# Twelve conditioning chunks split seven and five, and the last recurrent head's tail rearranged, in a one-layer diffusion backbone

## The chip, the cores and the metric

The kernel runs on one core of a Trainium2 chip. The metric is the device time of one execution in microseconds (us); the median of several executions counts.

## The reference, cut to what matters

One trunk layer is computed for 128 context tokens and 1024 latent tokens (1152 columns in all, in nine tiles of 128). The part around the change is this:

```python
mod = (silu(cond) @ ada_w + ada_b).reshape(2, 6, 1024)      # cond: c_ctx and c; ada_w is 1024 x 6144, 24 MB
sh1, sc1, g1, sh2, sc2, g2 = mod[:, 0..5]
h = rmsnorm(x, norm1) * (1 + sc1) + sh1                      # needs sh1 and sc1 only
aq, ak, av, rq, rf_f, rf_b, ri, rg, za, zr = split(h @ w_in)
# eight recurrent heads (HGRN2, both directions), key and value size 128
o_rec = rmsnorm(o_f + o_b, r_gain) * silu(rg)
merged = sigmoid(za) * attention + sigmoid(zr) * o_rec
x = x + g1 * (merged @ w_o)
h = rmsnorm(x, norm2) * (1 + sc2) + sh2                      # sh2, sc2, g2: used much later
x = x + g2 * conv_ffn(h)
```

## The kernel before, in words

Four phases follow one another, each in a block of its own with a barrier at its end: `phase0` (conditioning and the normalised, modulated, transposed input), `phase1` (eight recurrent heads), `phase2` (attention and output projection), `phase3` (the convolutional feed-forward part). Activations and weights are kept as a high part and a low part, and each projection is three matmul passes (lines 336 to 338) of 384 columns.

**Phase 0.** `ada_w` arrives in twelve chunks of 512 columns, 2 MB each, in three buffers (`AW`, line 177). A chunk's buffer is filled again when TensorE has read it. `columns(c)` (line 235) multiplies the two silu'd conditioning vectors, padded with zeros to 32 columns, by the chunk, 8 row blocks into four groups of 32 PSUM partitions. ScalarE copies the result to `mod_rows` (`MR`, line 215), and `rows(c)` (line 245) turns it by four tiny matmuls against `row_select` into columns of the modulation, which VectorE adds to the bias (line 300). Chunks 0 to 3 hold shift and scale of the first norm, chunks 4 to 11 the rest. From chunk 4 on, each chunk comes with one of the eight 128-row blocks of x (a "column" of x here), in three parts of 1, 4 and 4 token tiles: TensorE transposes the part (`x_part`, line 253), VectorE scales and shifts it into `h_f32` (`HF`, line 320), ScalarE rounds it to `act_hi` (`HH`, line 219), and VectorE subtracts to make `act_lo` (`HL`, line 312). ScalarE does the copy of chunk c (line 215) before the three parts that go with it. GpSimd splits the first three weight blocks (lines 188 and 190), which SP loads behind chunk 9 and at the end (lines 180 and 182). All of this is in written order on each engine, held together by semaphores.

**Phase 1.** The first head's six projection units (`unit(0, u)`, 18 groups of 24 matmuls) run on TensorE with nothing between them. GpSimd first clears the semaphores of phase 0 (`spent`, line 478 on) and then releases TensorE by adding to `w_split`. `gates(0)` on VectorE (lines 746 to 760) turns the forget gates into decays and writes `q_dec` and `k_dec`. Then a loop does the recurrence of head r between the projections of head r + 1. The last head has no projections beside it. Its tail: nine tiles of scores, masks (lines 795 to 801) and outputs; ScalarE copies each output tile to `rec_out` and its square to `SQ` (lines 647 and 648); three groups of 384 tokens are summed over the partitions by a matmul with ones (line 580), rooted on ScalarE (line 652), inverted on VectorE (line 812), multiplied into `rec_out` with the gain (line 814) and then with the gate (line 816). The gate is silu(rg) times sigmoid(zr), a product of 1152 columns on VectorE (line 805). One DMA stores all of `rec_out` (line 444), and the phase ends when it has landed.

Of the kernel before, what the change touches and what calls it, by code (L numbers as in the profile page):

```python
# [14 lines left out]
P = 128  # L15
D = 1024
KC = D // P
# [47 lines left out]
def build(nc, a, outs):  # L65
# [9 lines left out]
    with ExitStack() as ctx:  # L75
# [25 lines left out]

        W = (sb("w_raw", [P, 2, KC, P]), sb("w_hi", [P, 3, KC, P], F32R), sb("w_lo", [P, 3, KC, P], F32R))
        phase0(nc, a, sb, pb, sem, W, w_in, (B_RQ, B_RFF, B_RFB), HH, HL, ident, ones, CW, MOD, A1, A2, lb, lb1, lb1n, rgain)

        spent = sems[:]
        phase1(nc, a, sem, W, w_in64, HH, HL, ident, ones, lb, lb1, lb1n, rgain, w_in, rec_dram, out_state, spent)
# [7 lines left out]
def phase0(nc, a, sb_, pb_, sem, W, w_in, first_units, HH, HL, ident, ones, CW, MOD, A1, A2, lb, lb1, lb1n, rgain):  # L114

    with ExitStack() as ctx:
# [4 lines left out]
        NCOL = 12  # L121
# [8 lines left out]
        HF = sb("h_f32", [P, 2, 512])  # L130
# [3 lines left out]
        SEL = sb("row_select", [P, 2])  # L134
# [17 lines left out]
        xt_done, hf_done, hi_done, lo_done = sem("xt_done"), sem("hf_done"), sem("hi_done"), sem("lo_done")  # L152
# [3 lines left out]
        EARLY = 4  # L156
        X_FOR = {c: range(3 * (c - EARLY), 3 * (c - EARLY) + 3) for c in range(EARLY, NCOL)}
        ada = a["ada_w"][0].rearrange("(k p) (b c) -> b p k c", p=P, c=512)

        with nc.Block() as block:  # L160
            @block.sync
            def _(sp):
# [11 lines left out]
                for c in range(NCOL):  # L174
                    if c >= AHEAD:
                        sp.wait_ge(ada_done, c - AHEAD + 1)
                    sp.dma_start(AW[:, c % AHEAD], ada[c]).then_inc(ada_in[c % AHEAD], 16)
# [15 lines left out]
            def _(act):  # L193
# [5 lines left out]
                act.wait_ge(vec_ok, 1)  # L199
                nc.scalar.activation(SG[:, :], VT[:, 64:80], ACT.Sigmoid).then_inc(cond_sig, 1)  # L200
                act.wait_ge(vec_ok, 2)
                nc.scalar.activation(lb[:, :], LD[:, :], ACT.Sigmoid).then_inc(cond_sig, 1)
                for t in range(NT):
                    if t % 3 == 0:
# [5 lines left out]
                nc.scalar.activation(RS[:, :], SS[:, :], ACT.Sqrt).then_inc(sqrt_done, 1)  # L210
                for c in range(NCOL):
                    act.wait_ge(ada_done, c + 1)
# [3 lines left out]
                    for n in X_FOR.get(c, ()):  # L216
                        j, (t0, t1, _) = n // 3, GR[n % 3]
                        act.wait_ge(hf_done, n + 1)
                        nc.scalar.activation(HH[:, j, t0 * P:t1 * P], HF[:, n % 2, 0:(t1 - t0) * P], ACT.Copy).then_inc(hi_done, 1)

            @block.tensor
            def _(pe):
# [15 lines left out]
                def rows(c):  # L238
                    pe.wait_ge(ada_out, c + 1)
                    if c >= EARLY:  # L240
                        pe.wait_ge(vec_ok, 2)
                        pe.wait_ge(lo_done, 1)
                    out = mps if c < EARLY else vps
                    for b in range(4 * c, 4 * c + 4):
                        m = nc.tensor.matmul(out[:, 2 * b:2 * b + 2], MR[:, c % 2, (b - 4 * c) * P:(b - 4 * c + 1) * P], SEL[:, :], start=True, stop=True)
                    m.then_inc(mod_t, 1)

                def x_part(n):
                    j, (t0, t1, _) = n // 3, GR[n % 3]
                    if n >= 4:  # L250
                        pe.wait_ge(hf_done, n - 3)
# [6 lines left out]
                for c in range(1, EARLY):  # L258
                    columns(c)
                    rows(c - 1)  # L260
                rows(EARLY - 1)
                pe.wait_ge(xn_done, NT)
                for c in range(EARLY, NCOL):
                    for n in X_FOR[c]:
                        x_part(n)
                    columns(c)
# [2285 lines left out]
```

## Time and profile before

| | us |
|---|---|
| median of three runs | 2728.85 |
| lowest and highest | 2724.72, 2728.87 |
| the profiled execution, its own time | 2727.76 |
| its span in the profile | 2725.7 |
| TensorE busy (matmul) | 2586.0 (95%) |
| VectorE busy | 1705.9 (63%) |
| ScalarE busy | 1027.3 (38%) |
| GpSimd busy | 826.3 (30%) |

The profile is of one execution. Times in it are us from the start of the span, "busy" leaves out waiting, and a bracket at the end of a row of the timeline tells how long the engine had been idle and what released it. The matmuls are pipelined, so that the next one starts before the last one's end: the distance from start to start is what a matmul costs in a stream.

### The profile page before, as it was taken

How to read it: one execution, taken by the hardware profiler on the slowest of the kernel's cores; microseconds unless marked ns; L12 is line 12 of the kernel's file. 1: busy time of each engine (PE TensorE's matmuls, PEld its weight loads, DVE VectorE, ACT ScalarE, POOL GpSimd, SP SyncE). 2: the span in 40 equal slices, each digit the busy share in tenths (PEclk: the TensorE clock that was granted, in tenths of full speed). 3: DMA queues.
4: the chain of work that ended last, by engine and by line, in shares of the span. 5: the costliest groups of instructions: out<-in, count | busy, mean ns of one | idle time of the engine just before them, and what ended most of it. 6: DMA issues, size and time to landing. Idle time of an engine off the chain costs nothing. (4 is left out here: it accounts for less than half of the span.)

```text
span 2725.7 us, 40115 instructions
## 1 busy us (share of the span) xinstructions
PE 2586.0 (95%) x14417; PEld 2386.3 (88%) x14417; DVE 1705.9 (63%) x2809; ACT 1027.3 (38%) x1915; POOL 826.3 (30%) x775
## 2 busy tenths in 40 slices
PE   6899999999997999999999999799999999999997
PEld 2799999999997977778778676699999999999997
DVE  3247456546748367777677666437766777667675
ACT  3233323323323256666666657433122211222214
POOL 0222132223222433433433323624223222232222
PEclk8899999999999999999999999899999999999999
DMA  9411111111110200010010010411111111111101
GB/s 373 127 40 44 35 49 41 43 33 49 43 35 20 67 11 9 24 38 9 24 46 9 1 52 26 136 40 55 47 38 38 46 38 46 39 38 46 38 27 74
DMA packets 164250, 135.94 MB, mean 50 GB/s; under 512 B 18460, under 2 KB 141884, under 8 KB 164156
## 3 DMA queue, kind: packets, MB, share of 16 engines
q1 hardware_dynamic: 162940, 129.99, 15.2%
q10 hardware_dynamic: 1216, 4.72, 0.4%
q8 instruction: 56, 0.92, 0.1%
q14 instruction: 38, 0.31, 0.0%
HBM read 120.41 MB, written 14.29 MB: 49 GB/s over the span
## 5 line engine op out<-in xcount | busy, mean ns | idle before, releaser
L336 PE MATMUL proj_ps<-act_hi,w_hi 128*128 128x384 f32 x1152 | 409.8, 356 | 6.4 <-POOLq L478 6.4
L336 PE MATMUL ffn_ps<-act_hi,w_hi 128*128 128x384 f32 (+2 forms) x1128 | 384.6, 341 | 12.9 <-PEq L985 8.1
L338 PE MATMUL proj_ps<-act_hi,w_lo 128*128 128x384 f32 x1152 | 391.0, 339 | 0.0
L337 PE MATMUL proj_ps<-act_lo,w_hi 128*128 128x384 f32 x1152 | 390.6, 339 | 0.0
L338 PE MATMUL ffn_ps<-act_hi,w_lo 128*128 128x384 f32 (+2 forms) x1128 | 383.5, 340 | 0.0
L337 PE MATMUL ffn_ps<-act_lo,w_hi 128*128 128x384 f32 (+2 forms) x1128 | 383.4, 340 | 0.0
L2403 DVE SCALAR_TENSOR_TENSOR resid_t<-ffn_ps,mod,resid_t 128x384 f32<-128x384 f32 (+2 forms) x640 | 273.9, 510 | 139.3 <-PE ffn_ps L338 139.3
L1756 DVE TENSOR_TENSOR probs_lo<-att_ps,probs_hi 128x512 fp32r<-128x512 f32 x324 | 223.1, 689 | 157.5 <-ACT att_ps L1553 153.6
L1552 ACT ACTIVATE probs_hi<-att_ps 128x512 fp32r<-128x512 f32 x324 | 193.7, 598 | 198.7 <-PE att_ps L1372 197.8
L2381 DVE SCALAR_TENSOR_TENSOR conv<-up,conv_t,conv 128x127 f32<-128x127 f32 (+1 forms) x168 | 212.0, 1321 | 77.8 <-ACT conv L2309 66.0
L488 POOL CAST w_hi<-w_raw 128x1024 fp32r<-128x1024 f32 x48 | 75.2, 1567 | 558.3 <-PE proj_ps L338 525.8
L2082 POOL CAST w_hi<-w_raw 128x1024 fp32r<-128x1024 f32 x63 | 66.9, 1061 | 567.0 <-PE ffn_ps L338 567.0
L336 PEld LDWEIGHTS proj_ps<-act_hi,w_hi 128*128 128x128 f32 x1152 | 217.6, 189 | 9.3 <-POOLq L478 6.5
L336 PEld LDWEIGHTS ffn_ps<-act_hi,w_hi 128*128 128x128 f32 x1128 | 212.9, 189 | 14.5 <-issue 12.1
L337 PEld LDWEIGHTS proj_ps<-act_lo,w_hi 128*128 128x128 f32 x1152 | 217.6, 189 | 2.8
L338 PEld LDWEIGHTS proj_ps<-act_hi,w_lo 128*128 128x128 f32 x1152 | 217.0, 188 | 0.0
L337 PEld LDWEIGHTS ffn_ps<-act_lo,w_hi 128*128 128x128 f32 x1128 | 213.0, 189 | 0.1
L338 PEld LDWEIGHTS ffn_ps<-act_hi,w_lo 128*128 128x128 f32 x1128 | 212.8, 189 | 0.0
L1743 DVE TENSOR_REDUCE row_max<-att_ps 128x1 f32<-128x512 f32 x256 | 171.9, 686 | 50.6 <-PE att_ps L1358 47.0
L1553 ACT ACTIVATE att_ps<-att_ps 128x512 f32<-128x512 f32 x324 | 193.7, 598 | 0.0
L2315 ACT ACTIVATE gated_hi<-gated 128x1152 fp32r<-128x1152 f32 x20 | 23.3, 1167 | 388.2 <-DVE gated L2389 388.2
L336 PE MATMUL ffn_ps<-gated_hi,w_hi 128*128 128x384 f32 x480 | 160.7, 335 | 0.0
(291 smaller groups left out, 5725.0 us busy)
## 6 DMA issues: line engine op xcount, KB each, us to landing
w_raw<-in_w_in SPq DMA_DIRECT2D x64, 512.0 KB, 3.9
ada_w<-in_ada_w SPq DMA_DIRECT2D x12, 2048.0 KB, 13.8
w_raw<-in_w_up SPq DMA_DIRECT2D x44, 512.0 KB, 3.9
w_raw<-in_w_down SPq DMA_DIRECT2D x22, 512.0 KB, 3.6
rec_scratch<-rec_out SPq DMA_DIRECT2D x8, 576.0 KB, 2.8
out<-xy SPq DMA_DIRECT2D x9, 512.0 KB, 2.6
w_raw<-in_w_o SPq DMA_DIRECT2D x8, 512.0 KB, 6.1
xy<-in_x_sample SPq DMA_DIRECT2D x8, 512.0 KB, 6.6
```

Of the source, the lines that this page charges most:

```text
L336: nc.tensor.matmul(out, w_hi, x_hi, start=(k == 0), stop=False)
L337: nc.tensor.matmul(out, w_hi, x_lo, start=False, stop=False)
L338: return nc.tensor.matmul(out, w_lo, x_hi, start=False, stop=last)
L488: nc.gpsimd.tensor_copy(WH[:, u % 3], WR[:, u % 2]).then_inc(w_hi, 1)
L1552: nc.scalar.activation(PH[:, x % 4, :], bank, ACT.Exp, scale=SCALE)
L1553: nc.scalar.activation(bank, bank, ACT.Exp, scale=SCALE).then_inc(ex_done, 1)
L1743: m = nc.vector.tensor_reduce(MX[:, h:h + 1, part], bank, AX_X, ALU.max, negate=True)
L1756: nc.vector.tensor_tensor(PL[:, x % 4, :], ps[:, B_ST + x % 3, :], PH[:, x % 4, :].bitcast(F32), ALU.subtract).then_inc(lo_done, 1)
L2082: nc.gpsimd.tensor_copy(WH[:, s], WR[s]).then_inc(w_hi, 1)
L2315: nc.scalar.activation(GH[:, :], GF[:, :], ACT.Copy).then_inc(gh_ok, 1)
L2381: nc.vector.scalar_tensor_tensor(c, U[:, s, t0 + src:t0 + src + w], CW[:, tap, bass.ds(f + s * FB, 1)], c, ALU.mult, ALU.add).then_inc(tap ...
L2403: m = nc.vector.scalar_tensor_tensor(x, dn[:, n % RING, t0 - g * G:t1 - g * G], MOD[:, 40 + j, grp:grp + 1], x, ALU.mult, ALU.add)
```

## The change

1. Phase 0 handles seven chunks only, in the order 0, 2, 1, 3, 4, 5, 6. The two halves of shift and scale are formed separately, so columns 0 to 3 of x can start after chunks 0 and 2. The three parts of x per column are spread otherwise: ScalarE scales the third part of each column and rounds all three, VectorE scales two and makes three low parts, with three `h_f32` buffers in place of two. x's parts are no longer tied one column to one chunk. The loads of the first weight blocks stand behind chunk 3 and chunk 5. The two small sigmoids stand behind the sixth square.
2. Chunks 7 to 11 are handled in phase 1, within the first head's projections: one 2 MB buffer in the space of `q_dec` and `k_dec`, the columns matmuls after projection groups 1, 3, 5, 7 and 9, the rows matmuls after groups 2, 4, 6, 8 and 10. The stationary operand has two columns in place of 32, over a `scores_ps` cleared beforehand. VectorE adds them to the modulation within `gates(0)`.
3. GpSimd releases TensorE before it clears the old semaphores.
4. In the last head's tail the gate product and the gating of `rec_out` are GpSimd's, by group; sums, roots and inverses go by group between the tiles; each group is stored as it is ready.

```diff
+MOD_NOW, MOD_LATER = (0, 2, 1, 3, 4, 5, 6), (7, 8, 9, 10, 11)
...
-        NCOL = 12
+        NCOL = len(MOD_NOW)
-        X_FOR = {c: range(3 * (c - EARLY), 3 * (c - EARLY) + 3) for c in range(EARLY, NCOL)}
+        X_FOR = {3: range(0, 6), 4: range(6, 15), 5: range(15, 20), 6: range(20, NX)}
...
-                    if c == 9:
+                    if c == 3:
                         for u in range(2):
                             sp.dma_start(WR[:, u], w_in[first_units[u]]).then_inc(w_raw_in[u], 16)
-                sp.wait_ge(w_split, 1)
-                sp.dma_start(WR[:, 0], w_in[first_units[2]]).then_inc(w_raw_in[0], 16)
+                    if c == 5:
+                        sp.wait_ge(w_split, 1)
+                        sp.dma_start(WR[:, 0], w_in[first_units[2]]).then_inc(w_raw_in[0], 16)
...
+                def scaled_part(n):
+                    j, (t0, t1, grp) = n // 3, GR[n % 3]
+                    act.wait_ge(xt_done, n + 1)
+                    act.wait_ge(mod_ok, 3 if j < 4 else 6)
+                    if n >= 3:
+                        act.wait_ge(lo_done, n - 1)
+                    nc.scalar.activation(HF[:, n % 3, 0:(t1 - t0) * P], xps[:, n % 4, 0:(t1 - t0) * P], ACT.Identity,
+                                         scale=A1[:, j, grp:grp + 1], bias=MOD[:, j, grp:grp + 1]).then_inc(hf_done_a, 1)
...
+                def column_parts(j):
+                    high_part(3 * j)
+                    scaled_part(3 * j + 2)
+                    high_part(3 * j + 1)
+                    high_part(3 * j + 2)
+
+                parts_done = 0
                 for c in range(NCOL):
+                    while c in X_FOR and 3 * parts_done + 2 <= X_FOR[c][-1] - (3 if c + 1 < NCOL else 0):
+                        column_parts(parts_done)
+                        parts_done += 1
                     act.wait_ge(ada_done, c + 1)
...
                 columns(0)
+                columns(1)
+                rows(0)
+                rows(1)
+                for c in range(2, NCOL):
+                    if c == 3:
+                        pe.wait_ge(xn_done, NT)
+                    for n in X_FOR.get(c, ()):
+                        x_part(n)
+                    if c == 3:
+                        rows(2)
                     columns(c)
+                    if c == 3 or c > 4:
+                        rows(c if c == 3 else c - 1)
                 rows(NCOL - 1)
...
+                def load_chunk(i):
+                    if i:
+                        sp.wait_ge(ada_done, i)
+                    sp.dma_start(AW, ada[MOD_LATER[i]]).then_inc(ada_in, 16)
+
+                load_chunk(0)
+                load(0, 3)
+                load(0, 4)
                 first_states(0)
-                for u in range(3, NU):
-                    load(0, u)
-                for u in range(4):
+                load_chunk(1)
+                load(0, 5)
+                load_chunk(2)
+                load_chunk(3)
+                load(1, 0)
+                load_chunk(4)
+                for u in range(1, 4):
                     load(1, u)
...
-                store_rec(RH - 1)
+                for g in range(NG):
+                    sp.wait_ge(rec_ready, (RH - 1) * NG + g + 2)
+                    sp.dma_start(rec_dram[RH - 1][:, g * G:(g + 1) * G], OT[:, g * G:(g + 1) * G]).then_inc(rec_store, 16)
...
-                for done in spent:
-                    pool.sem_clear(done)
                 pool.sem_inc(w_split, C_SPLIT + 3)
...
+                for done in spent:
+                    pool.sem_clear(done)
...
+                pool.wait_ge(zr_sig, RH)
+                nc.gpsimd.tensor_tensor(RG[:, :], RG[:, :], ZR[:, :], ALU.mult).then_inc(last_gate, 1)
+                pool.wait_ge(last_gate, 1)
+                for g in range(NG):
+                    cols = slice(g * G, (g + 1) * G)
+                    pool.wait_ge(o_out, (RH - 1) * 2 * NT + 6 * (g + 1))
+                    nc.gpsimd.tensor_tensor(OT[:, cols], OT[:, cols], RG[:, cols], ALU.mult).then_inc(last_gated, 1)
...
+                def chunk_columns(i):
+                    if i == 0:
+                        pe.wait_ge(ada_zero, 1)
+                    pe.wait_ge(ada_in, 16 * (i + 1))
+                    if i >= 2:
+                        pe.wait_ge(ada_out, i - 1)
+                    for k in range(KC):
+                        q = k % 4
+                        m = nc.tensor.matmul(aps[32 * q:32 * q + 2, i % 2, :], C2[:, k, :], AW[:, k, :], start=(k < 4), stop=(k >= 4))
+                    m.then_inc(ada_done, 1)
...
                 for u in range(NU):
-                    unit(0, u)
+                    for g in range(NG):
+                        n = NG * u + g
+                        for part in range(3):
+                            unit_part(0, u, g, part)
+                        if n % 2 == 0 and 2 <= n <= 2 * len(MOD_LATER):
+                            chunk_rows(n // 2 - 1)
+                        if n % 2 and n < 2 * len(MOD_LATER):
+                            chunk_columns(n // 2)
...
                     outputs(r, j)
-                for g in range(NG):
-                    sum_squares(r, g)
+                    if j in (3, 6):
+                        sum_squares(r, j // 3 - 1)
+                sum_squares(r, 2)
...
                     out_evacuate(r, j)
-                for g in range(NG):
-                    norm_root(r, g)
+                    if j in (4, 7):
+                        norm_root(r, (j - 4) // 3)
+                norm_root(r, 2)
...
-                mask_scores(r)
-                gate_product(r)
-                normalise(r)
+                mask_scores(r, range(7))
...
+                invert(0, 0, G // 2)
+                mask_scores(r, (7,))
+                invert(0, G // 2, G)
+                mask_scores(r, (8,))
+                scale(0)
+                for g in (1, 2):
+                    invert(g, 0, G)
+                    scale(g)
```

`invert` is the reciprocal of line 812 over the given columns, `scale` the operation of line 814; `chunk_rows` is `rows` of phase 0 into `kv_ps`. On ScalarE the copy of each later chunk stands right behind the evacuation of projection groups 1, 3, 5, 7 and 9.

## Rows read from the trace of the kernel before

**Rows 1.** The page: TensorE's busy time over the whole span.

```profile
PE 2586.0 (95%) x14417; PEld 2386.3 (88%) x14417; DVE 1705.9 (63%) x2809; ACT 1027.3 (38%) x1915; POOL 826.3 (30%) x775
```

**Rows 2.** Windows: busy time by engine, granted clock, DMA share, GB/s.

```profile
40.00:60.00 20.00, 19.55 (x124) 11.29 (x116) 9.48 (x19) 6.02 (x12) 0.00 (x0) 0.74 1.05 386
...
100.00:120.00 20.00, 20.00 (x111) 20.00 (x111) 0.00 (x0) 3.25 (x5) 3.44 (x2) 0.96 0.20 54
```

**Rows 3.** Timeline of phase 0 and the start of phase 1, TensorE; start us, us, engine, line.

```profile
32.37 2.92 PE L235 MATMUL ada_ps<-ada_w,cond_silu 128*32 128x512 f32 x16 [1.16 <-DMA ada_w<-in_ada_w]
...
37.78 3.64 PE L235 MATMUL ada_ps<-ada_w,cond_silu 128*32 128x512 f32 x16 [0.70 <-DMA ada_w<-in_ada_w]
...
44.79 2.16 PE L253 MATMUL x_ps<-ident,x 128*128 128x128 f32 x9
...
55.83 1.92 PE L235 MATMUL ada_ps<-ada_w,cond_silu 128*32 128x512 f32 x16
...
57.68 1.05 PE L245 MATMUL vps<-row_select,mod_rows 128*128 128x2 f32 x8
...
71.61 1.92 PE L235 MATMUL ada_ps<-ada_w,cond_silu 128*32 128x512 f32 x16 [1.76 <-DMA ada_w<-in_ada_w]
...
96.40 0.69 PE L336 MATMUL proj_ps<-act_hi,w_hi 128*128 128x384 f32 x1 [6.39 <-POOLq L478]
```

**Rows 4.** The same timeline, VectorE.

```profile
28.25 6.05 DVE L297 TENSOR_SCALAR x<-x,rs 128x1024 f32<-128x1024 f32 x9
...
53.26 0.41 DVE L320 TENSOR_SCALAR h_f<-x_ps,a,mod 128x128 f32<-128x128 f32 x1
...
53.59 0.68 DVE L312 TENSOR_TENSOR act_lo<-h_f,act_hi 128x512 fp32r<-128x512 f32 x1
...
54.38 0.81 DVE L320 TENSOR_SCALAR h_f<-x_ps,a,mod 128x512 f32<-128x512 f32 x1
...
57.01 0.41 DVE L320 TENSOR_SCALAR h_f<-x_ps,a,mod 128x128 f32<-128x128 f32 x1
...
89.02 2.39 DVE L312 TENSOR_TENSOR act_lo<-h_f,act_hi 128x128 fp32r<-128x128 f32 x1 [0.16 <-ACT act_hi L219]
...
93.89 0.17 DVE L328 SCALAR_TENSOR_TENSOR a<-mod,vec_t 128x16 f32<-128x16 f32 x1
...
94.88 0.06 DVE L732 MEMSET eps_r<- 128x1 f32 x1 [0.82 <-PEq L160]
```

**Rows 5.** The same timeline, ScalarE.

```profile
55.22 0.63 ACT L219 ACTIVATE act_hi<-h_f 128x512 fp32r<-128x512 f32 x1 [0.94 <-DVE h_f L320]
```

**Rows 6.** The same timeline, GpSimd.

```profile
88.92 2.34 POOL L190 TENSOR_TENSOR w_lo<-w_raw,w_hi 128x1024 fp32r<-128x1024 f32 x1
```

**Rows 7.** The page, DMA issues: KB each, median us to landing.

```profile
ada_w<-in_ada_w SPq DMA_DIRECT2D x12, 2048.0 KB, 13.8
...
w_raw<-in_w_in SPq DMA_DIRECT2D x64, 512.0 KB, 3.9
```

**Rows 8.** Timeline of the change from head 0 to head 1, VectorE.

```profile
180.16 0.56 DVE L767 COPY keys_values_t<-t_o_ps 128x384 f32<-128x384 f32 x1 [7.92 <-PE t_o_ps L539]
```

**Rows 9.** Timeline of the last head's tail, VectorE.

```profile
870.19 1.36 DVE L805 TENSOR_TENSOR rg<-rg,zr 128x1152 f32<-128x1152 f32 x1
...
873.63 2.55 DVE L812 RECIPROCAL k_dec<-k_dec 128x384 f32<-128x384 f32 x1 [2.08 <-ACT k_dec L652]
...
876.21 0.62 DVE L814 SCALAR_TENSOR_TENSOR rec_out<-rec_out,rgain,k_dec 128x384 f32<-128x384 f32 x1
...
884.28 0.56 DVE L816 TENSOR_TENSOR rec_out<-rec_out,rg 128x384 f32<-128x384 f32 x1
```

**Rows 10.** The same timeline, ScalarE.

```profile
871.65 1.28 ACT L652 ACT_TABLE_LOAD   x1
```

**Rows 11.** The same timeline, TensorE.

```profile
870.99 1.46 PE L580 MATMUL kv_ps<-k_dec,ones 128*128 128x384 f32 x4
...
888.11 0.66 PE L1271 MATMUL att_ps<-w_hi,act_hi 128*128 128x384 f32 x1 [13.56 <-PEq L420]
```

More of the change, by code:

```diff
@@ L215, in _ @@
                     nc.scalar.activation(MR[:, c % 2, :], aps[:, c % 2, :], ACT.Copy).then_inc(ada_out, 1)
[L216 to L219, printed above, removed]
+                for j in range(parts_done, KC):
+                    column_parts(j)
             @block.tensor
@@ L239, in rows @@
                     pe.wait_ge(ada_out, c + 1)
-                    if c >= EARLY:
+                    if c >= 4:
                         pe.wait_ge(vec_ok, 2)
                         pe.wait_ge(lo_done, 1)
-                    out = mps if c < EARLY else vps
-                    for b in range(4 * c, 4 * c + 4):
-                        m = nc.tensor.matmul(out[:, 2 * b:2 * b + 2], MR[:, c % 2, (b - 4 * c) * P:(b - 4 * c + 1) * P], SEL[:, :], start=True, stop=True)
+                    out = mps if c < 4 else vps
+                    b0 = 4 * MOD_NOW[c]
+                    for b in range(b0, b0 + 4):
+                        m = nc.tensor.matmul(out[:, 2 * b:2 * b + 2], MR[:, c % 2, (b - b0) * P:(b - b0 + 1) * P], SEL[:, :], start=True, stop=True)
                     m.then_inc(mod_t, 1)
@@ L257, in _ @@
                 columns(0)
-                for c in range(1, EARLY):
-                    columns(c)
[L260 to L266, printed above, removed]
-                    if c > EARLY:
-                        rows(c - 1)
+                columns(1)
[8 more added lines that the diff above has]
+                        rows(2)
+                    columns(c)
+                    if c == 3 or c > 4:
+                        rows(c if c == 3 else c - 1)
                 rows(NCOL - 1)
@@ L580, in sum_squares, with chunk_rows @@
                     nc.tensor.matmul(kvps[:, g % 2, 0:G], ones[:, :], SQ[:, g * G:(g + 1) * G], start=True, stop=True).then_inc(ss_done, 1)
-                for u in range(NU):
-                    unit(0, u)
+                def chunk_columns(i):
[8 more added lines that the diff above has]
+                    m.then_inc(ada_done, 1)
+                def chunk_rows(i):
+                    pe.wait_ge(ada_out, i + 1)
+                    for b in range(4):
+                        n = 4 * i + b
+                        m = nc.tensor.matmul(kvps[:, 0, 2 * n:2 * n + 2], MR[:, i % 2, b * P:(b + 1) * P], SEL[:, :], start=True, stop=True)
+                    m.then_inc(mod_t, 1)
+                for u in range(NU):
+                    for g in range(NG):
[6 more added lines that the diff above has]
+                            chunk_columns(n // 2)
                 pe.wait_ge(zero_ok, 3)
+                pe.wait_ge(mod_ok, 1)
                 with pe.Fori(0, RH - 1) as r:
@@ L677, in rest_of_units, with behind @@
                     gate_exps(h, 1)
+                def behind(u, g):
+                    n = NG * u + g
+                    if n % 2 and n < 2 * len(MOD_LATER):
+                        chunk_evacuate(n // 2)
                 for g in range(NG):
                     evacuate(0, U_RQ, g, RQ, ACT.Silu)
+                    behind(U_RQ, g)
                 act.wait_ge(zero_ok, 3)
@@ L784, in chain_states, with mask_scores @@
                         assert count == [links(0, j), links(1, j)]
-                def mask_scores(r):
-                    for j in range(NT):
+                def mask_scores(r, tiles=range(NT)):
+                    for j in tiles:
                         dve.wait_ge(a_done, r * NT + j + 1)
```

116 lines of the change are left out of this document (82 added, 34 removed).

## The prediction

> **What bounds the kernel now.** I read the page first, then the windows, then the timeline of each engine where the diff touches it. TensorE is busy for 95% of the span [rows 1], so a saving counts where TensorE waits, and work added to TensorE counts in full unless it falls into a wait. The windows show two such places. In phase 0 the DMA engines are full (share 1.05, 386 GB/s) while TensorE runs short pieces at a low clock; from 100 us on TensorE is full and the DMA share is 0.20 [rows 2]. Phase 0 is set by the stream of chunks: the one at 37.78 is the fourth, that at 71.61 the tenth, so a 2 MB chunk takes (71.61 - 37.78) / 6 = 5.64 us, and TensorE waits for data before both [rows 3]. The first projection starts at 96.40, 2.3 us after VectorE's last operation (93.89 + 0.17), and it is released by GpSimd's queue, which clears semaphores then, while VectorE itself goes on 0.8 us after its last operation [rows 3, 4]. The second place is the tail of the last head: VectorE runs from 870.19 to 884.84 alone, and TensorE stands for 13.56 us until 888.11 [rows 9, 11].
>
> **Fewer chunks in phase 0.** Seven chunks in place of twelve take 28.2 us of transfer away. With the two weight loads of 512 KB (a quarter of a chunk, 1.4 us each) behind the fourth chunk and one behind the sixth, the last chunk lands at 37.8 + 3 x 5.64 + 3 x 1.4 = 58.9. SP and its queue keep up: each load waits for a buffer read some 10 us earlier. If the stream still set the end, columns (1.92), copy (0.6), rows (1.05) and one addition would end phase 0 at 62.8. I don't think that it does, because x's parts are next.
>
> **x's parts.** They start behind the third columns matmul, 32.37 + 2.92 = 35.3 [rows 3]; x is normalised by 34.3 even without the earlier squares [rows 4]. Now VectorE needs 57.01 - 53.26 = 3.75 us per column of x [rows 4]. ScalarE takes over one scaling of 0.81 (0.75 from start to start), which leaves 3.0. But the new order has a chain: scaling of the first part (0.33 to the next start), low part of the column before (0.79), second scaling (0.81), rounding on ScalarE (0.63), low part (0.68), with hops about 3.4 us [rows 4, 5]. I take 3.4; the ends are 3.0 and 3.75. Column 0 is done early, but ScalarE then stands before the copy of chunk 3, and TensorE reaches that chunk's columns only after six parts (18 transposes, 4.3 us at the pace of the nine at 44.79 [rows 3]), rows (1.05) and itself (about 3.3, between the 2.92 and 3.64 of the low clock): 43.9, copy until 44.4. Three columns of x and the halves' sums bring ScalarE to 55.0, with a short wait for chunk 4. Column 4: 58.4; then it waits for chunk 5's columns, which stand behind a transpose that needs the next column's buffer: 61.0. Columns 5 to 7 end on ScalarE at 69.8; copy, rows and addition 2.0: 71.8.
>
> GpSimd's three weight splits now fall into this stretch. A low part of 0.28 us takes 2.39 us while GpSimd's subtraction of 2.34 us runs [rows 4, 6]. Three of them cost between nothing and 7 us; two fall where VectorE waits anyway, so I add 3: the end is 74.8. The Trainium skill, page "SBUF — State Buffer", section "Who interferes with whom", says that a VectorE operation with two SBUF inputs and a GpSimd operation that reads SBUF exclude each other for a whole instruction; the row agrees. TensorE then starts 1.0 us later, not 2.3, since the clearing comes behind the release: 75.8 against 96.40, a gain of **20.6 us**. The bounds are 63.8 (the stream alone) and 83 (3.75 per column, 7 us of exclusion), gains of 32.6 and 13.
>
> **Five chunks in phase 1.** TensorE is full there [rows 2], so they have no cover. A chunk costs 57.68 - 55.83 = 1.85 for the columns and 1.05 for the rows at full clock [rows 3]: 2.9 x 5 = **14.5 us lost**. The bounds are 13 and, if every one ran at the low clock as at 37.78 (3.64) with rows at twice their time, 29; the stretch is dense, so I stay with 14.5. The page "TensorEngine Tiling (Array Packing)", section "Key Properties", of the Trainium skill says that a change of tiling mode drains TensorE. Columns of 32 and full width alternate in rows 3 too, so the 1.85 holds it; if it didn't, the sum would be worse by an amount that no run here shows.
>
> The buffer is single. A new chunk is asked for when the last has been read, and is wanted two projection groups and a rows piece later: 111 matmuls take 20 us [rows 2], so a group of 24 takes 4.3, and the sum is 9.6 us. Alone it should land 8.0 us after issue: 3.9 for 512 KB [rows 7] plus 1.5 MB more at the stream's pace, 4.2. So there is over 1 us of slack, and I charge nothing. SP is not held: the loads of the first head's later weights stand at places where their buffer isn't free before, and units 0 to 3 of head 1 are wanted more than 10 us after. GpSimd's queue gets the clears, but its first split waits for unit 0. On ScalarE a copy of 0.6 follows five evacuations, each of which has a group's 4.3 us to itself. `gates(0)` waits for the last rows with the key product only; VectorE has 7.92 us of idle time before head 1 now [rows 8], and TensorE comes 10 us or more later than the gates' start does, so that stays hidden.
>
> **The tail.** VectorE loses the gate product of 1.36 (not on the path: 2.08 of idle time follows it) and three gatings of 0.56; the first inverse (2.55) moves between the masks [rows 9]. Added on the path: one sum on TensorE (0.73) between the tiles [rows 11], and a wait of about 0.7 for the first root, since ScalarE loads its table (1.28) [rows 10] in the middle. From the last mask's old end at 870.2: 1.4 + 3 x 2.58 + 3 x 0.66 = 9.7 + 1.4, so 881.3 against 884.84. GpSimd's gatings take 2.34 x 384/1024 = 0.9 each and exclude masks or scalings for that time [rows 6]; one of three on the path, 0.9. The last store is a third as large, 0.5 less. Gain **3 us**; bounds 0 and 5. The product of 1152 columns runs beside the chain of states, which reads PSUM; it is hidden by nine tiles of work. By the rule of the Trainium skill cited above the blocked ones are the scalings and the last two steps of a mask, and the product beside the states is free.
>
> **The sum.** 20.6 - 14.5 + 3 = 9.1 us. The profiled execution took 2727.76 (span 2725.7, and 2.1 around it), so it would take 2718.7. The median of the runs is 1.1 above it: **2719.7**.
>
> **Rivals.**
> - *x's parts are the new bound, worse than I take them* (3.75 per column, more exclusion): gain in phase 0 of 13 to 16, net 2 to 5, 2724 to 2727. For it: ScalarE is in the chain twice now. Chance 0.15.
> - *The stream stays the bound*: end at 62.8 to 68, net 16 to 21, 2708 to 2713. For it: bare work is 3.0 per column. Against: the waits for copies in ScalarE's order. Chance 0.13.
> - *Slower: late reload of the single buffer.* It decides at `chunk_columns` 1 to 4, from 9.6 us between issue and landing; the net is a loss beyond 9.6 + 9.1/4 = 11.9. The rows bound it: the median landing of a chunk is 13.8, though in a queue of three [rows 7]; if 512 KB's 3.9 scaled with size it would be 15.6, a wait of 6.0 x 4 = 24, and 2744. Against: the stream's 5.64 per chunk. Chance 0.08.
> - *Slower: the two-column operand loses the overlap of four groups.* A sum of 384 columns at full width takes 0.73 [rows 11], 512 would take 0.97, eight of them 7.8 in place of 1.85: 30 us, net 2749. Against: the outputs still stand 32 partitions apart. Chance 0.04.
> - *The change doesn't do what it says*: chunk-free parts of x still wait for the copies in ScalarE's written order, so that each of chunks 3, 4 and 5 stops them for as long as before (some 5 us each in place of my 3 to 5 in all): net about 0, 2729. Chance 0.04.
>
> **How the numbers follow.** My own case has 0.56, with 2714 to 2724. About 0.2% (5.5 us) is what a measurement of this kernel can tell from no change. Faster by more: nearly all of my case and of the stream's, and a bit of the first rival, 0.74. Same: 0.14. Slower: 0.12. The range 2711 to 2728 takes in the first rival and half of the second, and leaves out the slow ones.
>
> **What would show it.** First projection at 74 to 78 us; VectorE waiting for ScalarE around 40 to 44 and 58 to 61; no wait of TensorE for the later chunks, 1.9 and 1.0 us for each in head 0; the last `rec_out` store issued 3 us closer to the last output, with a mask or scaling of 0.9 us more beside a gating. A first projection after 83, or DMA waits of over 2 us in head 0, would make it wrong.

## The result, and the profile after

The changed kernel takes **2692.07 us** (median; 2690.61 to 2694.43), the kernel before, on the same chip, 2726.78 (2724.16 to 2728.87). The ratio is 0.9874, 95% interval 0.9861 to 0.9888: 34.7 us less, where the forecast was 9 and its range ended at 2711. The profiled execution took 2690.61 with a span of 2688.7, 37.0 less than before. The experiments split this into about 13 us from the edits and 21 to 24 from something that the diff changes in passing: 96 bytes of new tensors stand ahead of the weights in SBUF.

Page of the kernel after, the lines that answer to rows 1 and 7:

```profile
PE 2560.2 (95%) x14417; PEld 2358.4 (88%) x14417; DVE 1699.5 (63%) x2807; ACT 1034.1 (38%) x1924; POOL 836.6 (31%) x779
...
w_raw<-in_w_in SPq DMA_DIRECT2D x64, 512.0 KB, 3.8
...
ada_w<-in_ada_w SPq DMA_DIRECT2D x7, 2048.0 KB, 15.5
...
q_k_dec<-in_ada_w SPq DMA_DIRECT2D x5, 2048.0 KB, 8.0
```

TensorE has exactly as many matmuls as before (14,417) and is busy for 25.8 us less [rows 1]. An edit that only removes waits can't do that. The late chunks land 8.0 us after issue, as estimated.

Timeline of the kernel after, TensorE, phase 0 and the first head:

```profile
38.85 1.92 PE L269 MATMUL ada_ps<-ada_w,cond_silu 128*32 128x512 f32 x16
...
52.56 3.64 PE L269 MATMUL ada_ps<-ada_w,cond_silu 128*32 128x512 f32 x16
...
60.19 3.42 PE L269 MATMUL ada_ps<-ada_w,cond_silu 128*32 128x512 f32 x16
...
76.17 0.41 PE L386 MATMUL proj_ps<-act_hi,w_hi 128*128 128x384 f32 x1 [1.15 <-ACTq L739]
...
86.23 1.90 PE L673 MATMUL scores_ps<-q_k_dec,cond_silu 128*2 128x512 f32 x16
...
92.33 0.95 PE L680 MATMUL kv_ps<-row_select,rec_out 128*128 128x2 f32 x8
...
97.48 1.90 PE L673 MATMUL scores_ps<-q_k_dec,cond_silu 128*2 128x512 f32 x16
```

The first projection starts at 76.17 (96.40 before [rows 3]); I had 75.8. The late columns have no wait on a DMA ahead of them, and take 1.90 and 0.95 us.

The same timeline, VectorE (L360 is the low part):

```profile
41.67 3.25 DVE L360 TENSOR_TENSOR act_lo<-h_f,act_hi 128x128 fp32r<-128x128 f32 x2 [0.96 <-ACT act_hi L235]
...
45.16 2.51 DVE L360 TENSOR_TENSOR act_lo<-h_f,act_hi 128x512 fp32r<-128x512 f32 x1
...
57.10 1.99 DVE L360 TENSOR_TENSOR act_lo<-h_f,act_hi 128x128 fp32r<-128x128 f32 x2 [2.10 <-ACT act_hi L235]
...
66.31 0.41 DVE L371 TENSOR_SCALAR h_f<-x_ps,a,mod 128x128 f32<-128x128 f32 x1
...
69.37 0.41 DVE L371 TENSOR_SCALAR h_f<-x_ps,a,mod 128x128 f32<-128x128 f32 x1
...
75.06 0.18 DVE L344 TENSOR_TENSOR mod<-vps,vec_t 128x24 f32<-128x24 f32 x1 [1.94 <-PE vps L280]
```

The same, GpSimd (its subtractions) and then ScalarE (the copies of a chunk's sums):

```profile
40.97 2.36 POOL L197 TENSOR_TENSOR w_lo<-w_raw,w_hi 128x1024 fp32r<-128x1024 f32 x1
...
44.45 2.67 POOL L197 TENSOR_TENSOR w_lo<-w_raw,w_hi 128x1024 fp32r<-128x1024 f32 x1
...
55.98 2.36 POOL L197 TENSOR_TENSOR w_lo<-w_raw,w_hi 128x1024 fp32r<-128x1024 f32 x1
```

```profile
40.84 0.60 ACT L251 ACTIVATE mod_rows<-ada_ps 128x512 f32<-128x512 f32 x1 [1.98 <-PE ada_ps L269]
...
56.27 0.60 ACT L251 ACTIVATE mod_rows<-ada_ps 128x512 f32<-128x512 f32 x1 [3.60 <-PE ada_ps L269]
...
63.69 0.60 ACT L251 ACTIVATE mod_rows<-ada_ps 128x512 f32<-128x512 f32 x1 [4.91 <-PE ada_ps L269]
```

At three places low parts are stretched by GpSimd's subtractions (two of 0.28 take 3.25 together, one of 0.68 takes 2.51, and two of 0.28 take 1.99), a column of x takes 69.37 - 66.31 = 3.06 us when nothing else is in the way, and ScalarE stands 3.60 and 4.91 us for the columns of chunks 4 and 5.

The last head's tail after, VectorE, and then ScalarE, GpSimd and TensorE:

```profile
850.28 0.53 DVE L937 TENSOR_TENSOR masked_scores<-masked_scores 64x64 f32<-64x64 f32 x1
...
854.73 1.35 DVE L972 RECIPROCAL q_k_dec<-q_k_dec 128x192 f32<-128x192 f32 x1 [0.73 <-ACT q_k_dec L763]
...
860.38 2.55 DVE L972 RECIPROCAL q_k_dec<-q_k_dec 128x384 f32<-128x384 f32 x1
...
866.21 0.62 DVE L978 SCALAR_TENSOR_TENSOR rec_out<-rec_out,rgain,q_k_dec 128x384 f32<-128x384 f32 x1
```

```profile
852.82 1.28 ACT L763 ACT_TABLE_LOAD   x1
```

```profile
849.74 1.00 POOL L584 TENSOR_TENSOR rec_out<-rec_out,rg 128x384 f32<-128x384 f32 x1 [7.18 <-ACT q_k_dec L759]
...
861.36 0.99 POOL L584 TENSOR_TENSOR rec_out<-rec_out,rg 128x384 f32<-128x384 f32 x1 [5.26 <-ACT q_k_dec L759]
```

```profile
837.44 1.16 PE L633 MATMUL kv_ps<-keys_values_t 128*128 128x128 f32 x8 [0.58 <-ACT keys_values_t L748]
...
869.17 0.66 PE L1426 MATMUL att_ps<-w_hi,act_hi 128*128 128x384 f32 x1 [6.77 <-PEq L479]
```

From the first product of the state chain to the first matmul of phase 2 the tail takes 869.17 - 837.44 = 31.7 us. Before, the same chain started at 851.61 and the matmul at 888.11 [rows 11]: 36.5. The wait is 6.77 in place of 13.56.

So far everything is close to what was forecast. The rest is found by laying the marks side by side: from the first projection to the chain of the last head the kernel before needs 851.61 - 96.40 = 755.2 us, the one after 837.44 - 76.17 = 761.3, though it has 14 us more to do there; and from phase 2 to the end, where the diff changes no line, they need 1837.6 and 1819.5. The groups of matmuls by form (the last numbers are busy us, mean ns, idle us) show it; before first, then after:

```profile
L337 PE MATMUL proj_ps<-act_lo,w_hi 128*128 128x384 f32 x1152 | 390.6, 339 | 0.0
...
L337 PE MATMUL ffn_ps<-act_lo,w_hi 128*128 128x384 f32 x1096 | 372.5, 340 | 0.0
...
L337 PE MATMUL ffn_ps<-gated_lo,w_hi 128*128 128x384 f32 x480 | 160.5, 334 | 0.0
```

```profile
L387 PE MATMUL proj_ps<-act_lo,w_hi 128*128 128x384 f32 x1152 | 386.7, 336 | 0.0
...
L387 PE MATMUL ffn_ps<-act_lo,w_hi 128*128 128x384 f32 x1096 | 367.0, 335 | 0.0
...
L387 PE MATMUL ffn_ps<-gated_lo,w_hi 128*128 128x384 f32 x480 | 160.3, 334 | 0.0
```

ScalarE's evacuations of a projection, one for each group of 24 matmuls, show the same as a pace; before, then after:

```profile
158.31 0.49 ACT L633 ACTIVATE zr<-proj_ps 128x384 f32<-128x384 f32 x1 [3.75 <-PE proj_ps L338]
162.55 0.49 ACT L633 ACTIVATE zr<-proj_ps 128x384 f32<-128x384 f32 x1 [3.75 <-PE proj_ps L338]
```

```profile
150.88 0.49 ACT L744 ACTIVATE zr<-proj_ps 128x384 f32<-128x384 f32 x1 [3.67 <-PE proj_ps L388]
155.04 0.49 ACT L744 ACTIVATE zr<-proj_ps 128x384 f32<-128x384 f32 x1 [3.67 <-PE proj_ps L388]
```

### The profile page after: what moved, and what is told of

Same layout as the page of the kernel before. It is cut to its first block and busy times, and to the rows that moved or that the text cites. A ratio compares the mean times of both kernels' runs of the same rounds, so it can differ in the third digit from the quotient of the medians.

```text
span 2688.7 us, 40126 instructions
## 1 busy us (share of the span) xinstructions
PE 2560.2 (95%) x14417; PEld 2358.4 (88%) x14417; DVE 1699.5 (63%) x2807; ACT 1034.1 (38%) x1924; POOL 836.6 (31%) x779
## 5 line engine op out<-in xcount | busy, mean ns | idle before, releaser
L386 PE MATMUL ffn_ps<-act_hi,w_hi 128*128 128x384 f32 (+2 forms) x1128 | 378.7, 336 | 13.3 <-PEq L1140 8.1
L387 PE MATMUL ffn_ps<-act_lo,w_hi 128*128 128x384 f32 (+2 forms) x1128 | 377.8, 335 | 0.0
L388 PE MATMUL ffn_ps<-act_hi,w_lo 128*128 128x384 f32 (+2 forms) x1128 | 377.7, 335 | 0.0
```

The costliest lines, as they stand in the source:

```text
L386: nc.tensor.matmul(out, w_hi, x_hi, start=(k == 0), stop=False)
L387: nc.tensor.matmul(out, w_hi, x_lo, start=False, stop=False)
L388: return nc.tensor.matmul(out, w_lo, x_hi, start=False, stop=last)
```

## The experiments

A kernel whose ratio is given was compared with the kernel before on the same chip in the same session. "Distance" is that from `act_hi` to `w_hi` (`act_lo` and `w_lo` keep their places beside them, so theirs are it too up to multiples of 512).

**1. The kernel before, weights moved by 32 bytes.**

```diff
+        sb("pad_w", [P, 8])
         W = (sb("w_raw", [P, 2, KC, P]), sb("w_hi", ...
```

> The kernel before with one unused tensor of 32 bytes per partition ahead of w_raw, so that w_raw, w_hi, w_lo and all that lies behind them start on a multiple of 64 bytes (they start 32 bytes past one before); act_hi and act_lo stay on a multiple of 64. Placement theory (the missing 25 us come from where the tensors lie in the on-chip memory, which the change moved by 96 bytes): 2726.8 - 25 = about 2702 us, with a group of 24 projection matmuls 4.16 us apart in place of 4.24. Rival (the faster pace comes from the rearranged instructions): 2727 us and 4.24.

Measured: 2702.48 us (2698.68 to 2705.09), ratio 0.9906 (0.9889 to 0.9922), from an allocation that nothing uses. The placement is real, and it is most of the surprise.

**2. The changed kernel with the same pad.**

> The changed kernel with the same unused tensor of 32 bytes, which puts w_raw and all behind it 32 bytes past a multiple of 64 again. Placement theory: about 2692 + 25 = 2717 us, near the predicted 2719.7, with groups 4.24 us apart. Rival (rearranged instructions): 2692 us and 4.16.

Measured: 2694.93 (2693.88 to 2696.91), ratio 0.9876 (0.986 to 0.9893). A miss: `w_hi` is off the multiple of 64 again, and the kernel is fast. The theory that the weights' own alignment counts falls.

**3. and 4. The kernel before with the activations moved, alone and with the weights.** The pad stands ahead of `act_hi`, so that all tensors move together (3); in 4 there is the pad of 1 as well.

```diff
+        sb("pad_first", [P, 8])
         HH = sb("act_hi", [P, KC, T], F32R)
```

> The kernel before with the 32 bytes ahead of act_hi: act_hi and act_lo now start 32 bytes past a multiple of 64, the weights and all else on a multiple. If only the weights' own start counts: about 2702 us as in the run with the weights alone moved. If it counts that the streamed operand and the weights start alike: act projections are as slow as before, about 2722 to 2727 us. If the streamed operand's own start counts: slow too, and the two last are told apart by the run with both moved.

> The kernel before with 32 bytes ahead of act_hi and 32 more ahead of w_raw: activations, weights and all else start 32 bytes past a multiple of 64. If it counts that both start alike: about 2702 us. If each operand's own start counts: 2727 us or more.

Measured: 3 takes 2723.76 (2722.27 to 2725.5), ratio 0.9983 (0.9973 to 0.9992), and its matmuls 339 and 340 ns as before; 4 takes 2706.41 (2705.25 to 2709.12), 0.9916 (0.9899 to 0.9932). In 3 `w_hi` has the address of 1 and the distance of before, and it is slow. In 4 the distance is that of 1 at other addresses, and it is fast. The distance counts.

**5. The changed kernel with its two tensors behind the weights.**

```diff
-        C2, SEL = sb("cond_silu2", [P, KC, 2]), sb("row_select", [P, 2])
         W = (sb("w_raw", [P, 2, KC, P]), sb("w_hi", ...
+        C2, SEL = sb("cond_silu2", [P, KC, 2]), sb("row_select", [P, 2])
```

> The changed kernel with its two small new tensors allocated behind the weights' buffers in place of ahead of them, so that w_hi and w_lo start where they did before (84384 bytes behind act_hi, in place of 84480). Nothing else differs. If the distance between the activations and the weights makes the pace: 2692 + 25 = about 2717 us, and then the change itself is worth 2729 - 2717 = 12 us, near the 9.1 predicted. If the place is not it: 2692.

Measured: 2716.43 (2715.77 to 2719.02), ratio 0.9967 (0.9953 to 0.9981). With the old distance the change brings 12 us by the medians (9 by the ratio, 5 to 13 by its interval), not 35.

**6. to 8. Other distances, in the kernel before.** 6 allocates `rgain` behind the weights (distance 84,352), 7 `lb1n` and `rgain` (84,288), 8 `ones` (83,872, 512 less than before).

> The kernel before with rgain allocated behind the weights: the distance from act_hi to w_hi falls by 32 bytes to 84352, both on a multiple of 64. If 84384 is slow because the two starts differ by an odd multiple of 32: fast here, about 2703 us. If it is slow because of the distance itself, of which 84416, 84480 and 84512 are the fast side: slow or slower here, 2727 us or more.

> The kernel before with lb1n and rgain behind the weights: distance 84288, 96 bytes less than before. It shows how wide the slow band is: 2727 or more if it goes on, 2703 if it ends.

> The kernel before with ones (512 bytes) behind the weights: distance 83872, that is 84384 - 512. Weights and activations are both read in pieces whose starts differ by multiples of 512 bytes. If only the rest of the distance by 512 counts: as slow as before, 2727 to 2729 us. If it is a longer period or this one distance: faster.

Measured: 2723.98 (2722.85 to 2725.68), ratio 0.9988 (0.9977 to 0.9998); 2716.97 (2714.5 to 2720.34), 0.9962 (0.9951 to 0.9973); 2727.76 (2725.69 to 2730.91), 1.0001 (0.9991 to 1.0012). Moving by 512 bytes changes nothing.

**9. The changed kernel without chunks 7 to 11.** It leaves out their loads, products and sums, so that the first gate and the second norm's shift, scale and gate keep their biases alone.

> The changed kernel without its work on chunks 7 to 11 in the first head: no loads, no columns and rows matmuls, no copies of them; gate 1 and the second norm's shift, scale and gate keep their biases alone. It gives the price of the five chunks. By the prediction 14.5 us (2.9 each), so about 2692 - 14.5 = 2677.5 us. Rival: they are partly free or cost waits too, under 10 or over 18 us.

Measured: 2677.86 (2674.5 to 2678.96), ratio 0.9816 (0.9799 to 0.9832): 14.2 us less than the changed kernel, with an interval of some 4 us on each side. In the trace the chain of the last head starts at 822.54 with the first projection at 75.88, 14.6 us less between the two than in the changed kernel (761.3). The chunks cost what the columns and rows cost, and nothing waits for them. The last head's tail starts 14.9 us sooner, and of this 12.6 arrive at the end.

**10. The changed kernel with the old tail**: gate product, gating and one inverse after another on VectorE, one store.

> The changed kernel with the last head's tail as it was before: gate product, gating, sums, roots and inverses in the old order on the old engines, one store. By the prediction the new tail is worth 3 us, by the trace's restart of TensorE after the last output 4.8: 2695 or 2697 us. Rival: the shorter tail is given back later in the next phase, 2692.

Measured: 2699.02 (2698.04 to 2700.86), ratio 0.9898 (0.9881 to 0.9914), 7 us more than the changed kernel, with an interval of some 4 us on each side. The trace, TensorE:

```profile
872.94 0.66 PE L1396 MATMUL att_ps<-w_hi,act_hi 128*128 128x384 f32 x1 [13.55 <-PEq L479]
```

The chain starts at 836.47 there: 36.5 us, as before, against 31.7. So the tail is worth 4.8. The rest of the 7 us is within the interval.

**11. The changed kernel with the clears ahead of the split**, in the order of before.

```diff
                 def _(pool):
+                for done in spent:
+                    pool.sem_clear(done)
```

> The changed kernel with GpSimd clearing the old semaphores ahead of the release of TensorE, as before. By the prediction 1.3 us slower (2693.4), seen as a first projection 1.3 us later behind the last VectorE operation of phase 0; the difference is below what three rounds can tell, the profile has to show it.

Measured: 2695.21 (2693.1 to 2697.23), ratio 0.9885 (0.9868 to 0.9901). Its TensorE:

```profile
76.06 0.69 PE L386 MATMUL proj_ps<-act_hi,w_hi 128*128 128x384 f32 x1 [2.62 <-POOLq L551]
```

VectorE's last operation starts at 73.47, 2.6 us before it; in the changed kernel 76.17 - 75.06 = 1.1. Clearing behind the release is worth 1.5 us; the rest of the 3 is within the interval.

**12. The changed kernel with the copies of chunks 4 and 5 earlier in ScalarE's order**, and with x's parts and the columns and rows matmuls of TensorE ordered accordingly.

```diff
-        X_FOR = {3: range(0, 6), 4: range(6, 15), 5: range(15, 20), 6: range(20, NX)}
+        X_FOR = {3: range(0, 6), 4: range(6, 10), 5: range(10, 16), 6: range(16, 21)}
```

> The changed kernel with another written order in phase 0: the columns matmuls of chunks 4, 5 and 6 come after fewer parts of x (10, 16 and 21 in place of 15, 20 and 24), the rows of chunk 3 later, and ScalarE takes every column of x whose parts are transposed before it waits for a chunk. If the waits of ScalarE for the chunks' columns (in the changed kernel 3.6 us before 56.27 and 4.9 us before 63.69) are the cost of tying x to the chunks, the first projection comes 4 to 6 us earlier and the time falls to 2686 to 2688. If VectorE's own work or the exclusion by GpSimd sets the pace, under 1.5 us are gained, 2690.5 or more.

Measured: 2692.02 (2691.51 to 2692.57), ratio 0.9871 (0.9854 to 0.9887). The first projection and phase 2 come sooner, the end doesn't:

```profile
71.64 0.66 PE L388 MATMUL proj_ps<-act_hi,w_hi 128*128 128x384 f32 x1 [3.14 <-ACTq L741]
```

Phase 2 starts at 865.32, 3.9 us before that of the changed kernel. These are the windows from the start of phase 2 to the end, first of this kernel, then of the changed one:

```profile
865.32:2689.30 1823.98, 1750.04 (x9358) 1590.26 (x9358) 1220.05 (x1972) 751.00 (x1398) 617.05 (x669) 0.98 0.13 39
```

```profile
869.17:2688.70 1819.53, 1745.82 (x9358) 1586.77 (x9358) 1220.63 (x1972) 752.45 (x1398) 616.95 (x669) 0.99 0.13 40
```

The same 9358 matmuls take 4.2 us more of TensorE at a mean granted clock of 0.98 in place of 0.99. The difference lies in short stretches: in 920 to 980 us the clock is 0.94 against 0.97, in 1460 to 1540 0.96 against 0.99, in 1860 to 1940 0.98 against 1.00. So in this pair of profiles the gain of phase 0 was given back by the clock. That the edit does this isn't shown. Kernels with the same distances differ as much in this stretch, in one profile each: 1819.5 us in the changed kernel, 1821.0 in run 9, 1821.8 in run 11, 1823.6 in run 10, 1824.0 in run 12 and 1824.5 in run 13. Over all four executions the mean clock is 0.985 in the changed kernel and 0.984 here. The medians show no gain, but each ratio has an interval of some 4 us on each side, so a gain of 4 us isn't ruled out either.

**13. to 15. The map of distances completed, in the kernel before.** 13 and 14 have the pad of 1 with 96 and 224 bytes (distances 84,480, as in the changed kernel, and 84,608); 15 allocates `lb1`, `lb1n` and `rgain` behind the weights (84,224).

> The kernel before, with 96 unused bytes ahead of w_raw, so that w_hi lies 84480 bytes behind act_hi, as in the changed kernel (0 modulo 512). If this distance alone is the missing part of the change, it takes as much off the kernel before as it took off the changed one: 24.4 us, so about 2703 of 2728. If the gain in the changed kernel needed its other edits too, it stays above 2715.

> The same with 224 bytes: distance 84608, 128 modulo 512. If the slow distances are one band around 384 to 416, it is as fast as at 0: 2702 to 2706. If several bands repeat within 512 bytes, it may be slow: 2720 or more.

> lb1, lb1n and rgain allocated behind the weights: distance 84224, 256 modulo 512. The run at 320 gave 2717, half of the gain. If the band has its lower edge there, 256 gives 2702 to 2710. If the loss repeats every 256 bytes, 256 acts like 0 and is fast as well, but then 128 (like 384) is slow.

Measured: 13 takes 2706.17 (2704.33 to 2708.24), ratio 0.9922 (0.9906 to 0.9939); 14 takes 2722.82 (2721.73 to 2724.16), 0.9984 (0.9974 to 0.9993); 15 takes 2712.52 (2711.29 to 2712.97), 0.9945 (0.9929 to 0.9962). The changed kernel's distance alone takes 21 us off the kernel before (16 to 26 by the ratio's interval). One band within 512 bytes was the wrong picture: 128 is as slow as 384 (run 6). And 15 is slower than 13 for a reason that its groups of matmuls show:

```profile
L337 PE MATMUL ffn_ps<-act_lo,w_hi 128*128 128x384 f32 x1096 | 367.6, 335 | 0.0
...
L337 PE MATMUL ffn_ps<-gated_lo,w_hi 128*128 128x384 f32 x480 | 163.1, 340 | 0.0
```

Here the gated matmuls are the slow ones: moving tensors behind the weights had changed the distance from `w_hi` to `gated_hi`. The same holds for 5, 6 and 7. All runs together, distances modulo 256, ns of the matmuls with `act_lo` (heads, feed-forward) and `gated_lo`, and us from the first projection to the end of the profiled span:

```
kernel          act to w  heads ffn    w to gated  gated   to the end
13              0         336   335    0           334     2607.6
15              0         335   335    160         340     2613.1
7               64        338   337    96          339     2620.4
14              128       338   339    0           334     2624.8
6               128       338   339    32          337     2626.7
before, 3       160       339   340    0           334     2629.3, 2629.4
8 (512 less)    160       339   340    0           334     2629.8
1, 4            192       337   338-9  0           334-5   2605.7, 2609.3
after           0         336   335    0           334     2612.5
2               32        338   338    0           335     2616.9
5               160       339   340    96          339     2638.5
16              160       339   340    0           334     2637.2
```

The last four are the changed kernel with its chunks. Two pairs of operands that have nothing to do with each other follow one rule: 334 to 336 ns where the distance is a multiple of 256 bytes, 338 to 340 at 96 to 160, 337 to 339 at 32, 64 and 192. Run 1 is the one that fits worst: its matmuls are slower than those of 13, and it ends 2 us sooner. The last column is of one profile for each kernel, and by run 12 such a stretch differs by some 5 us between kernels of the same distances.

A third pair settles whether the streamed operand alone could be the cause. `w_units` lies as far from `act_hi` modulo 256 as `w_hi` does, except where tensors were put between the two: then 0 in run 5 and 160 in run 15, while `w_hi` is at 160 and at 0. The same stream then has two paces in one kernel, first run 5, then run 15:

```profile
L387 PE MATMUL ffn_ps<-act_lo,w_hi 128*128 128x384 f32 x1096 | 372.6, 340 | 0.0
...
L387 PE MATMUL ffn_ps<-act_lo,w_units 128*128 128x384 f32 x120 | 40.1, 334 | 0.0
```

```profile
L337 PE MATMUL ffn_ps<-act_lo,w_units 128*128 128x384 f32 x120 | 40.6, 338 | 0.0
```

One group doesn't show the rule. In phase 2 the weights stream against `act_hi` and `act_lo` (864 matmuls); the middle pass takes 342 ns before, 343 in run 13 with the changed distance, and 340 in the changed kernel, in 15 and in 16. Whether the rule fails there or the clock hides it stays open.

**16. The changed kernel with all distances of before.** The two tensors stand ahead of `act_hi`, so everything moves together.

```diff
+        C2, SEL = sb("cond_silu2", [P, KC, 2]), sb("row_select", [P, 2])
         HH = sb("act_hi", [P, KC, T], F32R)
```

> The changed kernel with the two new tensors allocated ahead of act_hi: every later tensor moves by the same 96 bytes, so the distances from act_hi to w_hi (84384, 160 modulo 256) and from w_hi to gated_hi (0 modulo 256) are those of the kernel before. Putting them behind the weights had also moved gated_hi to 96 modulo 256 from w_hi, and its matmuls took 339 ns in place of 334. If the pace of a matmul follows the distance between its two operands modulo 256, then here proj and ffn take 339 to 340 ns, the gated ones 334, and the time shows the edits alone: 10 to 14 us less than before, with the 5 us that the gated matmuls lost no longer in it, so 2709 to 2714. If the operands' own addresses matter, the gated ones stay at 339 and the time is 2716 again. My prediction's sum, 9.1 us, would give 2718.6.

Measured: 2715.54 (2714.01 to 2717.05), ratio 0.9955 (0.9941 to 0.9968). The matmuls do what the rule says:

```profile
L387 PE MATMUL proj_ps<-act_lo,w_hi 128*128 128x384 f32 x1152 | 390.3, 339 | 0.0
...
L387 PE MATMUL ffn_ps<-gated_lo,w_hi 128*128 128x384 f32 x480 | 160.5, 334 | 0.0
```

The time is 1.5 us above the range that I gave, and only 0.9 below run 5 where I expected some 5 (3.3 by the two ratios); that part is unexplained, though within the intervals. This is the fair value of the edits: **13.2 us** by the medians (12.3 by the ratio, 8.7 to 16.1 by its interval). Runs 13 and 16 split the change in two: the distance alone has a ratio of 0.9922, the edits alone 0.9955, and their product, 0.9877, is within the interval of the whole change (0.9874). So the two add up. Its marks on TensorE:

```profile
75.64 0.66 PE L386 MATMUL proj_ps<-act_hi,w_hi 128*128 128x384 f32 x1 [1.30 <-ACTq L739]
...
876.93 0.66 PE L1426 MATMUL att_ps<-w_hi,act_hi 128*128 128x384 f32 x1 [6.26 <-PEq L479]
```

## Why the prediction was wrong, point by point

**The step that failed** is the sum itself: "20.6 - 14.5 + 3 = 9.1 us" takes everything outside the three edited stretches as unchanged. The diff has a fourth edit that no part of the prediction costs: two allocations ahead of the weights. By run 13 they alone are worth 21 us in the kernel before, by run 16 against the changed kernel 2715.5 - 2692.1 = 23, more than all the rest. With the distances kept, the kernel takes 2715.5, which lies in the forecast's range of 2711 to 2728. None of the rivals named a pace of the matmuls either.

**Phase 0**: 20.6 forecast, 96.40 - 76.17 = 20.2 measured, 20.8 in run 16. The sum is right, its terms less so. The transposes and columns of chunk 3 ran at the full clock (1.92, not 3.3; the granted clock is 1.00 from 38.85 to 40.80), and its copy started at 40.84, 3 us sooner than I had it. The exclusion with GpSimd cost (3.25 - 0.56) + (2.51 - 0.68) + (1.99 - 0.56) = 6.0, twice my 3 and near the upper bound of 7. A column of x takes 3.06, not 3.4. The waits of ScalarE for chunks 4 and 5 are 3.60 and 4.91 us, from 52.7 and from 58.8 on, where I had a short wait and 58 to 61: their columns ran at or near the low clock (3.64 at a granted clock of 0.50, 3.42 at 0.55). VectorE waited for ScalarE for 0.96 us before 41.67, 2.10 before 57.10 and 3.79 before 64.51. Columns 5 to 7 of x were done at 72.3 in place of 69.8, with the exclusion in it. The end of VectorE's last operation, 75.24, was forecast as 74.8, and the 1.0 of the release is 0.9. The rival of a stream that stays the bound is out: run 12 shows that the written order on ScalarE and TensorE was the bound, and that the first projection could start 4.5 us sooner.

**Five chunks**: 14.5 forecast, 14.2 (run 9's time) and 14.6 (its trace) measured, 1.90 + 0.95 for one. Neither slow rival came: chunks land in 8.0 us against the 9.4 at hand (97.48 - 86.23 - 1.90; I had 9.6), and the two-column operand keeps the overlap of its four groups (1.90 against 1.92 with 32 columns). The drain at a change of tiling mode, which I cited from the Trainium skill ("TensorEngine Tiling (Array Packing)", "Key Properties"), is not seen as a cost beside these durations.

**The tail**: 3 forecast, 36.5 - 31.7 = 4.8 measured (4.1 in run 16). VectorE ends 3.8 us sooner after the chain's start; I had 3.5, less 0.9 for exclusion, of which only one mask operation shows any (0.53 in place of 0.22). Two of GpSimd's gatings lie beside a reciprocal, which is not stretched: one within that at 860.38, 2.55 us as before [rows 9], the other within the half at 854.73, 1.35 us like the half that has no gating beside it. The first root's wait for its table is 0.73 as forecast. The last store, a third of the old one, brings 0.9 in place of 0.5: TensorE starts 2.3 us after VectorE's end, not 3.3. `gates(0)` stayed hidden, as forecast.

**Around the median**: 1.1 us between the profiled execution and the median of before was added; it is within what runs differ by.

**What would have shown it.** My conditions for being wrong were a first projection after 83 and DMA waits in the first head. Neither came, and the forecast was wrong all the same: I had named no condition for a gain outside the edited stretches. One was to be had from the diff and the trace of before: a group of 24 takes 4.24 us in the heads, while the gated matmuls, of the same form, took 334 ns against 340.

## What to carry to other kernels

Read a diff for its allocations too: each tensor put ahead of others moves them, and where two of them stream against each other for most of the span, 1% hangs on it. Before an edit is judged, run it with the distances of the kernel before, or the kernel before with those of the edit; and once the best distance is known, set it on purpose. A gain at one place should be followed to the end, with the granted clock of the later stretches beside it: in its profile run 12 brought 4 us to the start of phase 2 and none to the end, and whether its edit or the spread between executions took them back isn't shown.

## What the runs showed of the hardware

- A matmul of 128x384 whose weights and whose streamed operand lie a multiple of 256 bytes apart in their partitions takes 334 to 336 ns, one at 96 to 160 modulo 256 takes 338 to 340; from start to start the group of 24 takes 4.16 and 4.24 us. It holds for `act_hi`/`w_hi`, `act_hi`/`w_units` and `gated_hi`/`w_hi`, and moving both operands (run 3) or one by 512 bytes (run 8) leaves these times as they are. In phase 2, where the weights stream, it doesn't show. What in the chip does this isn't shown; no run tells reads of the weights apart from reads of the stream.
- With twelve chunks the end of phase 0 isn't steady: in eight of the ten kernels with the old phase 0 the first projection starts at 95.3 to 96.4, but in run 1 at 90.92 and in run 3 at 93.57. With seven chunks, where x's parts set the end, it starts at 75.0 to 76.2 in all runs with the changed order. So the gain of phase 0 depends on the profile that it is taken against, by up to 5.5 us, and a part of the difference between runs of equal distances (1 and 4: 2702.5 and 2706.4) may come from there. What delays or hastens the old phase 0 wasn't tried.
- VectorE's low parts, with two SBUF inputs each, took 1.4 to 2.7 us longer beside GpSimd's subtractions (one, or two together); reciprocals, with one input, took no longer beside GpSimd's gatings (1.35 and 2.55 us). This agrees with the rule of the Trainium skill ("SBUF — State Buffer", "Who interferes with whom") that I cited.
